# A two-block transformer kernel in fp32 on one core: the first block's attention is put in another order, with twelve dense tiles in quarters between its score tiles

## What is computed

```python
proj = rms_norm(x, attn_norm[l]) @ w_in[l]
h_mla, h_diff, h_ch = jnp.split(proj, [IN_MLA, IN_MLA + IN_DIFF], axis=-1)
o_mla = rms_norm(mla_attention(h_mla, positions, ...), mla_out_norm[l])       # 6 heads, 96-wide keys with rotation
o_diff = diff_attention(h_diff, positions, ..., slopes)                       # 6 heads, two score maps each
o_ch = rms_norm(chunk_attention(h_ch, chunk_rel_bias[l]), chunk_out_norm[l])  # 4 heads, with a bias table
x = x + jnp.concatenate([o_mla, o_diff, o_ch], axis=-1) @ w_out[l]
x = x + conv_ffn(rms_norm(x, ffn_norm[l]), ...)

# diff_attention, one block of 128 queries
s = jnp.einsum('bqhmd,bkhmd->bmhqk', qb, k).astype(jnp.float32) * scale
s = s - slopes[None, None, :, None, None] * dist[:, None, None]               # ALiBi: slope times distance
s = jnp.where(chunk_causal_mask(start, S), s, -jnp.inf)
p = jax.nn.softmax(s, axis=-1)
a = p[:, 0] - lam_full * p[:, 1]
```

## Time and profile before

| | us |
|---|---|
| median of three runs | 3296.06 |
| lowest, highest | 3293.13, 3297.18 |
| the profiled execution, by its own time | 3294.52 |
| its span, first to last instruction | 3292.8 |
| mean granted TensorE clock | 0.957 |

### The profile page before, as it was taken

One profiled execution on the slowest core, in us unless ns is written; L12 is line 12 of the kernel. 1 busy time (PEld: TensorE's weight loads), 2 busy tenths in 40 slices (PEclk: granted clock), 3 DMA queues, 4 the chain that ended last, 5 costly groups with the idle time before them and its releaser, 6 DMA issues.

```text
span 3292.8 us, 40404 instructions
## 1 busy us (share of the span) xinstructions
PE 3120.4 (95%) x14074; PEld 2445.6 (74%) x14074; DVE 1385.8 (42%) x3077; ACT 841.7 (26%) x1855; POOL 1366.3 (41%) x924
## 2 busy tenths in 40 slices
PE   7999999999989999989999989999799999899997
PEld 6656788887656788878666768888686667688885
DVE  4575443343774434343741741112437417411123
ACT  2346221122455212121333321101213333210012
POOL 4210455554210555555223445555352234455552
PEclk9988999999989999999999989999899999899998
DMA  7310466665311666655223546666452235466662
GB/s 248 102 52 26 153 188 196 194 207 185 103 39 36 190 193 191 193 183 179 90 90 116 154 153 192 185 192 205 127 179 90 90 113 156 144 190 190 199 198 90
DMA packets 136518, 494.00 MB, mean 150 GB/s; under 512 B 15280, under 2 KB 15536, under 8 KB 136112
## 3 DMA queue, kind: packets, MB, share of 16 engines
q0 software_dynamic: 66240, 241.20, 24.1%
q1 hardware_dynamic: 68544, 245.40, 23.3%
q10 hardware_dynamic: 1584, 5.33, 0.5%
HBM read 489.77 MB, written 2.10 MB: 149 GB/s over the span
## 4 chain that ended last, share of the span: by engine, by line
PE 91%; DVE 5%; issue 2%; ACT 2%; DMA 1%; POOL 0%; SPq 0%; DVEq 0%; POOLq 0%
PE ps L468 25%; PE ps L469 23%; PE ps L470 23%; PE ps L621 6%; PE ps L644 5%; PE ps L634 2%; PE ps L577 1%; PE ps L579 1%; PE ps L578 1%; PE ps L531 1%; PE ps L540 1%; DVE ps L916 1%; DMA x<-xt 1%; DVE lo L931 0%; ACT sq L1394 0%
## 5 line engine op out<-in xcount | busy, mean ns | idle before, releaser
L468 PE MATMUL ps<-hi,w_hi 128*128 128x512 f32 x3216 | 1288.7, 401 | 39.8 <-POOL w_lo L444 15.0
L469 PE MATMUL ps<-hi,w_lo 128*128 128x512 f32 x3216 | 1263.3, 393 | 0.0
L470 PE MATMUL ps<-lo,w_hi 128*128 128x512 f32 x3216 | 1262.7, 393 | 0.0
L444 POOL TENSOR_TENSOR w_lo<-w_raw,w_hi 128x1024 fp32r<-128x1024 f32 x460 | 1107.3, 2407 | 82.9 <-DMA w_hi<-weights 73.8
L439 POOL DMA_DIRECT2D w_hi<-weights x460 | 262.6, 571 | 1796.1 <-PE ps L470 1654.1
L468 PEld LDWEIGHTS ps<-hi,w_hi 128*128 128x128 f32 x3216 | 610.3, 190 | 232.3 <-issue 87.7
L470 PEld LDWEIGHTS ps<-lo,w_hi 128*128 128x128 f32 x3216 | 609.9, 190 | 130.7
L469 PEld LDWEIGHTS ps<-hi,w_lo 128*128 128x128 f32 x3216 | 611.0, 190 | 120.6
L977 DVE CUSTOM_DVE_ANT_0 pr<-ps,kc 128x128 f32<-128x128 f32 (+1 forms) x208 | 88.9, 427 | 344.8 <-PE ps L621 343.3
L1456 ACT ACTIVATE pT<-ps 128x128 f32<-128x128 f32 (+1 forms) x248 | 97.8, 394 | 370.8 <-PE ps L634 370.7
L1602 ACT ACTIVATE ps<-hb,col 128x512 f32<-128x512 f32 x88 | 68.5, 782 | 381.1 <-DVE hb L960 381.1
(11 more groups left out here) (269 smaller groups left out, 3155.7 us busy)
## 6 DMA issues: line engine op xcount, KB each, us to landing
w_raw<-weights SPq DMA_DIRECT2D x460, 512.0 KB, 3.5
w_hi<-weights POOLq DMA_DIRECT2D x460, 512.0 KB, 3.9
x<-xt SPq DMA_DIRECT2D x8, 256.0 KB, 16.8
out<-x SPq DMA_DIRECT2D x8, 256.0 KB, 2.0
kc<-k ACTq DMA_DIRECT2D x1, 1216.0 KB, 5.2
bias<-relb ACTq DMA_DIRECT2D x2, 512.0 KB, 15.9
bias<-relb ACTq DMA_DIRECT2D x1, 1024.0 KB, 4.9
praw<-pt ACTq DMA_DIRECT2D x2, 512.0 KB, 3.4
```

Source lines behind the costliest of these rows:

```text
L444: nc.gpsimd.tensor_tensor(wlo[s][:, :], raw[s][:, :], whi[s][:, :].bitcast(F32), ALU.subtract).then_inc(w_split, 1)
L468: nc.tensor.matmul(out_ap, w[0], xx[0], start=first, stop=False)
L469: nc.tensor.matmul(out_ap, w[1], xx[0], start=False, stop=False)
L470: return nc.tensor.matmul(out_ap, w[0], xx[1], start=False, stop=last)
```

## The change

- Before the attention stand only two dense tiles (`dq0`, `dk0`) and the values. The sums of the input come straight after the two tiles, the spreading after the first unit of values (`between=first_spread`). They use banks 2 and 3.
- Twelve tiles lie in the attention, as quarters at `it` 0 to 23: two at each, except none at 12 and 15 and four at 13 and 14. The weight stream has the new order.
- The tasks are in another order: differential heads 0 and 1, chunk heads 0 and 1, differential heads 2 to 5, the six MLA heads, chunk heads 2 and 3.
- The sums of `cc` are at 12, their spreading at 15, the rotation of `kr` at 20. The thirteen small tiles (Q, K, V) are at 24 to 36, in an order in which each head gets its own in time. The single wait at 38 is gone; instead the scores of a head's first task wait for that head's tile, rotation and key copy, and the value products wait for their value tile.
- The output norms: differential sums at 39, spreading at 43 and 45; MLA sums at 61, spreading at 64; the chunk outputs are last, after the attention (`chunk_factors`, after six of eight chunks).
- ALiBi: the ScalarE tables and their semaphore are gone. The query is divided by the slope when it leaves PSUM (one scalar_tensor_tensor in the place of a tensor_tensor), the distance table is stored negative with the mask, and L977 adds it for every head; the exponential's scale is the slope.
- In layer 0 the distance table is made before the factors of the input norm. The angles are made in VectorE's `side(2)`, the sines in ScalarE's `side(3)`, the sine's sign in VectorE's `side(5)`. The bias table is prepared in `side(0)` and `side(1)`, in both layers.
- The early probability slots are used for 25 tasks instead of 20.

```diff
+ORDER_1 = ["cq0", "ck0", "cc0", "cc1", "cc2", "dq1", "stats", "dk1", "kr", "sp0", "sp1", "dq2", "dk2", "cq1", "ck1",
+           "Q0", "K0", "Q1", "V0", "V1", "Q2", "Q3", "K1", "Q4", "Q5", "K2", "V2", "V3",
+           "ds", "do0", "do1", "do2", "ms", "mo"]
+ITEM_AT = {24: "Q0", 25: "K0", 26: "Q1", 27: "V0", 28: "V1", 29: "Q2", 30: "Q3", 31: "K1", 32: "Q4", 33: "Q5", 34: "K2",
+           35: "V2", 36: "V3"}
...
-        EARLY = 20
+        EARLY = 25
...
-                                   add=alibi[a][h][:, off:off + n], coef=-slope / DIFF_QK ** -0.5,
-                                   alibi=DIFF_H * l + h + 1))
+                    d.append(Task(maps, n, "diff", diff_slope(h), [vd[:, kb, h * 64:h * 64 + 64] for kb in range(qb + 1)],
+                                  64 * (h % 2), dq[h // 2], qb, h % 2 == 0 and qb == 0, h % 2 == 1 and qb == NTB - 1,
+                                  add=dist[:, off:off + n], after=after))
...
+            return d[0:8] + c_[0:8] + d[8:24] + m_ + c_[8:16]
...
-        FULL_END = [2 * j + 1 for j in range(8)]
-        AT_STATS, AT_SPREAD, AT_Q, AT_K, AT_V, AT_READY = 16, 19, 23, 29, 32, 38
-        AT_DIFF, AT_CH, AT_OUT, AT_OUT2, AT_MLA = 41, 45, 48, 50, (52, 59)
+        QUARTERS = {it: 2 for it in range(24)}
+        QUARTERS.update({12: 0, 13: 4, 14: 4, 15: 0})
+        FULL_END = [1, 3, 5, 7, 9, 11, 13, 14, 17, 19, 21, 23]
+        AT_STATS, AT_SPREAD, AT_KR = 12, 15, 20
+        AT_DIFF, AT_OUT, AT_OUT2, AT_MLA, AT_MOUT = 39, 43, 45, 61, 64
...
+                        if t.more.get("kcopy"):
+                            pe.wait_ge(kcopy, t.more["kcopy"])
+                        for tile_n in t.more.get("after", ()):
+                            pe.wait_ge(d_free[BANK[tile_n]], USE[tile_n] + 1)
...
                 dense(2, A, NC_, need)
-                input_norm()
-                dense(1, A, NC_)
-                input_spread()
-                dense(3, A, NC_)
-                values(4, 2, 384, A, need, natural)
+                q.sq += NC_
+                first_sums()
+                values(4, 2, 384, A, need, natural, first_spread)
                 values(2, 4, 256, A, need, natural)
...
-                    elif it == AT_READY:
-                        pe.wait_ge(rope_done, q.rope * 7)
-                        pe.wait_ge(kcopy, q.kcopy * 6)
...
-                dense(8, A, NC_, need, (5, mla_factors))
+                dense(8, A, NC_, need, (6, chunk_factors))
...
+                def query(i, bank):
+                    return V.scalar_tensor_tensor(out=dq[i][:, :], in0=ps[:, bank, :], scalar=kc1[:, K1["qs"] + i:K1["qs"] + i + 1],
+                                                  in1=rx[:, :], op0=ALU.mult, op1=ALU.mult)
...
+                    if it < 2:
+                        if it == 0:
+                            dve.wait_ge(aux_in, 64 + 16 * l)
+                        for h in (2 * it, 2 * it + 1):
+                            V.scalar_tensor_tensor(out=bias[:, h, :], in0=bias[:, h, :], scalar=CH_HD ** 0.5,
+                                                   in1=kc1[:, 0:S], op0=ALU.mult, op1=ALU.add)
+                    elif l == 0 and it == 2:
+                        angles()
+                    elif l == 0 and it == 5:
+                        signed_sine()
...
-                def slope_times_distance(h):
-                    A_(alibi[a][h][:, :], dist[:, :], ACT.Copy,
-                       scale=TASKS["1", l][NTB * h].more["coef"]).then_inc(alibi_ready, 1)
...
+                    if l == 0 and it == 3:
+                        act.wait_ge(tab_ready, tabs + 1)
+                        A_(sin1[R, :], sin1[R, :], ACT.Sin).then_inc(tab_act, 1)
+                        A_(cos1[R, :], cos1[R, :], ACT.Sin).then_inc(tab_act, 1)
```

454 lines of the change are left out of this document (255 added, 199 removed).

## The result

The changed kernel takes 3304.64 us (median of its runs, 3293.63 to 3312.05) against 3294.76 for the kernel before on the same chips. The ratio is 1.0037, 95% interval 1.0029 to 1.0046. It is slower by 0.4% where 0.9% faster was predicted, and lies outside the range of 3230 to 3290.

The account below looks back on a forecast made before the run. TensorE, busy 95% of the span, was taken as the bound, so only its waits and low-clock stretches could give time. -16.1 - 18.4 + 2.6 + 1 = -30.9 against 3294.5 gave 3263.6, as a median 3265 us; range 3230 to 3290.

Parts of the forecast that it names:

- Part 1: Ahead of the attention: four dense tiles leave the front, taking 21.4 us a layer off it, and come back inside as quarters.
- the 1.5 for the distance table: Layer 0's front: the distance table, now ahead of VectorE's reading of the sums, was to cost 1.5 us, mostly hidden.
- The lower clock: Each layer's attention: full clock almost everywhere, falls at the start and after pauses remaining in part, an estimated 6 us added.
- Norms about 8: Iterations 37 to the end: the norms of the outputs were to take about 8 us of that stretch's 55.0.
- VectorE beside the small tiles: Iterations 24 to 30: VectorE's differential tasks and two rotations, 23.3 us, up to 28 with collisions, against TensorE's 22.8; 28 taken.
- Part 3: Layer 0's tables: 5.9 us of pause go, angles inside the attention cost 7, the distance table 1.5; net +2.6 us.
- Part 4: The remaining small edits, including ALiBi, waits per head, one more root and changes of table: +1 us over both layers.
- The waits per head: Waits replacing the single one at iteration 38 were to cost nothing, as keys are finished four iterations or more ahead.
- The added root: One more root a layer, 2.6 us of ScalarE where it has 2.9 to spare in a head: +1 us over both layers.
- Lower clock stays through 24 to 36: Rival, chance 0.1: the clock falls at iteration 24 and isn't given back, +24 us a layer, 3313 us, slower by 0.5%.
- The cover holds fully: Rival, chance 0.2: VectorE keeps up in iterations 16 to 36 and the clock stays up, 17 us less a layer, 3230.
- Gain eaten in small pieces: Rival, chance 0.08: stalls at iterations 12 to 16 and VectorE behind until 36, each 5 us a layer more, 3285 to 3292.

## Why the prediction was wrong

**Part 1 was right.** The front gave 21.3 us in layer 1 (21.4 said) and 28.5 in layer 0 (21.4 + 5.9 - 1.5 = 25.8 said). The pause between the `vd` and `vc` units fell from 6.6 to 0.7, as said. The 2.7 more than said is a fall of the clock too: in the front of before the lower clock holds from 78.12 to 84.95 us, right across the end of that pause (80.36), and after there is no such stretch, which is worth 3.4 us. So here too the pause had been priced without its fall, this time to the change's good, and the 1.5 for the distance table isn't seen.

**The lower clock is the step that failed.** "The fall at the start and after pauses will remain in part; I add 6 us" against "84 us at 0.66 to 0.79 now". Three things were wrong in it. The 84 us were not all at the lower clock: by the earlier trace rows 23.7 and 20.5 us of them were, worth 22 us together if nothing else limits. Second, the sum priced nearly every stretch from rows at clock 1.00 (0 to 6 alone came from a row at 0.95) and put the falls into one estimate that came from no row. Third, it took the fall for a property of the bare stretches 16 to 36, which filling would end. Filling did end most of it there (44.4 and 41.0 us at the lower clock before, 17.1 and 20.5 after), and the sign that the prediction had set, a clock of 0.9 or more in 16 to 36, came out at 0.91 and 0.90; but the falls in 0 to 15 and from 37 on, which no sign watched, made up for it. After the change 54.6 us of each attention run at 1.2 GHz, that is 27.3 us lost, where 6 stood: 21.3 short a layer. The attention became 32.8 and 24.0 us longer where +12.3 (with the tables) and +3.0 were said, so the whole miss in it is 20.5 and 21.0. All other terms together were therefore right within about 1 us, but not each one:

| stretch, layer 1 | forecast | after | of it lost to clock, by PEclk |
|---|---|---|---|
| 0 to 6 | 33.4 | 34.2 | 1.7 |
| 7 to 14 | 42.0 | 48.5 | 5.2 |
| 15 to 23 | 3.7 + 44.4 | 49.1 | 3.4 |
| 24 to 30 | 28 | 32.2 | 6.8 |
| 31 to 36 | 19.5 | 20.1 | 0 |
| 37 to the end | 55.0 | 71.1 | 10.3 |

(Half of the time at the lower clock counts as lost.) Without the clock the first five stand at 32.5, 43.3, 45.7, 25.4 and 20.1 and were at most 3 us off. The last one is 60.8 against 55.0, 5.8 too low without any fall. 2.4 of that is the end put too early (in the rows of before as well, so that it is no part of the miss); the rest is about what the MLA norm costs, which now has nothing beside it: leaving it out shortens the last 9.6 us to 6.0, a part of that by the clock. "Norms about 8" was a sum of busy times, and the price of a norm in a bare tail is the chain of its steps.

**VectorE beside the small tiles.** I saw that the rotations would set the pace there (28 us) and gave them only their own length. Leaving them out gives back 19 us, and in the two profiled executions 6 us a layer are won in 37 to 46, behind the last rotation. That TensorE's pauses in 24 to 36 are released by the rotations was half right: of 8.6 us in layer 0 the trace puts 4.3 to VectorE's maxima, but of 6.4 in layer 1 only 1.4, the others to ScalarE's copies (1.5 and 2.2) and to nothing that it shows (2.8 each). The collision with GpSimd at 37 was not in the sum: I had counted collisions up to iteration 30, and had not asked when the small tiles' units come free.

**The sign of the fill.** Filling the bare tasks 16 to 23 raised the clock as hoped, 0.65 to 0.93, and gained 1.4 to 2.8 us a layer. The bare stretch had 19.2 us at the lower clock, worth 9.6, and TensorE's 2.45 us of idle time; the quarters brought a pause behind the rotation (2.24) and 6.5 us at the lower clock.

**Part 3, the angles:** +7 said. 40.3 in layer 0 against 34.15 in layer 1 makes +6.2, with the pause of 5.02 us in the 2 to 6 that were named. The size was right, and the experiment shows that nothing had to be paid: ahead of the attention they cost nothing that can be seen.

**Part 4.** The waits per head show no pause of their own. The added root lies at iteration 62, in the tail, not where ScalarE had room; its share of the 4 to 7 us that the norm costs was not measured apart. The Trainium skill, "ScalarE: Activation LUTs", section "What ACT_TABLE_LOAD costs", gives a drain of about 1380 ns besides the load. The trace of after again shows none behind the load (and ScalarE's copy ahead of it ended at 321.14, so none there either):

```profile
321.16 1.28 ACT L1638 ACT_TABLE_LOAD   x1
322.45 0.21 ACT L1638 ACTIVATE small<-small 128x4 f32<-128x4 f32 x1
```

**The rivals.** "Lower clock stays through 24 to 36" had the mechanism and the sign (3313), and the wrong place: in layer 1 24 to 30 ran at 0.79, 31 to 36 at 1.00, and most of the falls lay outside. The range stopped at 3290 all the same, although this rival with its 0.1 stood above it. For the rival "The cover holds fully" the prediction read that TensorE's share is 100% wherever quarters lie; its own rows have 33.60 of 34.75 us in iterations 0 to 6 and 5.99 of 7.79 in the one behind the rotation. "Gain eaten in small pieces" named the squares at 12 and VectorE until 36, and gave each 5 us; with the falls behind them that is about what they cost. It had 0.08. Both together had 0.18, and a case for both at once wasn't there. The chance of slower, 0.09, was read off one mechanism with a high bar (two thirds of one stretch), while the same loss spread over several stretches needed no bar at all. The sign of the result was thus missed by the mechanism, not by bad luck: 20 executions each, and 10 us between the medians.

## What to carry to other kernels

Price the clock as a term of its own from the rows: twice (1 - g) times the length is the time at the lower level, half of that is the most that the clock can give back there, and a plan that makes new thin places and pauses elsewhere spends it again. Count each pause that the new order makes at its length plus half of the fall that may stand behind it: here 4.35 us for a pause of 1.13 and 5.66 for one of 2.24, but only 1.15 for the same 1.13 in the other layer and 4.65 for one of 5.02. And compare clocks over many executions, not over two profiles. Before dense work is laid into an attention, look at what stands ahead of the maximum on VectorE: placing its side work (rotations, angles, sums) where VectorE has slack was worth 32 us here, and the dense tiles themselves 1.4 to 2.8 us a layer.

## What the runs showed of the hardware that I had not expected

- Behind a pause of 1.13 us on TensorE and 24 one-column sums the clock fell, although dense work at full pace stands on both sides (851.49 to 877.39, clock 0.80), and with the quarters put ahead of the sums the same 129 records of iterations 12 to 15 ran at 0.93 instead of 0.82. In layer 0 the fall stayed with the pause gone (0.87 and 0.87).
- A fall can begin when the pause is over and outlast it: the pause of 2.24 us ended at 909.14, the lower clock holds from 909.55 to 916.38, and the first dense matmuls in it have records of 0.63 us against 0.40. The one beside the angles began inside the pause (81.88 to 86.90; lower clock from 83.52 to 90.35).
- Not every pause has a fall: those of 1.71, 0.86, 0.84 and 0.69 us in iterations 33 to 36 of layer 1 lie in a stretch at 1.00 (958.64 to 978.72).
- Extra dense matmuls in a thin stretch cost less than half of their own time (10 us for 21.4), since part of it comes back by the clock and part lies in pauses; in the last 15 us of layer 0's attention 4.0 us of them made the stretch 0.8 us shorter.
- The same 119 records of TensorE with 2.7 and 2.5 us of idle time ran once at 1.00 (25.85 us) and once at 0.78 (31.07 us).
- Executions of one kernel scatter by 4 to 10 us in their time at the lower clock, and the longer ones are those with more of it.
